# First two expert blocks turned by a one-hot product of x instead of a gather, in a two-layer block kernel on one Trainium2 core

## The reference, cut to what matters

```python
xn = rmsnorm(x, norm2_g)                    # [512, 1024]; x times 1/rms of its row times a gain
logits = xn @ w_router + b_router           # 4 groups, then 8 experts in the best group
top two experts of each token, with softmax weights
xs = xn[row_tok]                            # tokens sorted by expert, in blocks
ys = (silu(xs @ w_gate[e]) * (xs @ w_up[e])) @ w_down[e]     # 32 experts, hidden width 512
out = x + sum over a token's two experts of weight * ys
```

## Time and profile before

| | |
|---|---|
| runs, median of 3 | 1725.02 us (1723.73 to 1726.02) |
| the profiled execution, its own time | 1727.39 us |
| its span in the trace | 1725.5 us |
| PE busy | 1634.2 us, 95% |
| DVE busy | 742.6 us, 43% |
| ACT busy | 378.8 us, 22% |
| POOL busy | 191.5 us, 11% |
| HBM read and written | 298.60 MB and 15.73 MB |

### The profile page before, as it was taken

How to read it: one execution, slowest core, us unless ns; L and a number is a source line. 1 busy time by engine, 2 the same in 40 slices (tenths; PEclk the granted TensorE clock), 3 DMA queues, 4 the chain that set the end, 5 groups by cost and what they waited for, 6 DMA issues and landing times.

```text
span 1725.5 us, 17923 instructions
## 1 busy us (share of the span) xinstructions
PE 1634.2 (95%) x6932; PEld 943.7 (55%) x6932; DVE 742.6 (43%) x1517; ACT 378.8 (22%) x810; POOL 191.5 (11%) x206
## 2 busy tenths in 40 slices
PE   7999999999999999999999999997799998888986
PEld 4444454578888888855444788444333333333332
DVE  3386886465445454343774555256221211111111
ACT  4443754410000000022563223002111111010110
POOL 0000000000000000010002323150122211121211
PEclk9999999999999999999999999998799999998998
DMA  5531114030222212222121104539699999999993
GB/s 184 125 71 49 50 50 147 1 110 12 87 98 98 92 56 97 98 69 92 50 73 64 58 28 135 195 104 416 245 361 400 403 409 403 400 394 418 400 404 114
DMA packets 69089, 304.51 MB, mean 176 GB/s; under 512 B 10735, under 2 KB 11892, under 8 KB 55948
## 3 DMA queue, kind: packets, MB, share of 16 engines
q1 hardware_dynamic: 60416, 287.40, 43.1%
q0 software_dynamic: 7840, 13.80, 3.8%
q10 hardware_dynamic: 748, 2.15, 0.3%
HBM read 298.60 MB, written 15.73 MB: 182 GB/s over the span
## 4 chain that ended last, share of the span: by engine, by line
PE 85%; DMA 12%; DVE 2%; issue 1%; ACT 0%; POOL 0%; POOLq 0%; SPq 0%; DVEq 0%; ACTq 0%
PE ps L1589 11%; PE ps L1151 11%; PE ps L1195 11%; PE ps L1019 8%; PE ps L1292 7%; DMA W<-in_w_expert_up 6%; PE ps L1439 5%; PE ps L1604 5%; PE ps L1055 3%; PE ps L1015 3%; PE ps L1478 3%; PE ps L1504 2%; DMA yT<-in_w_expert_up 2%; DMA mix<-in_w_expert_up 2%; PE ps L1303 2%; PE ps L1074 1%
## 5 line engine op out<-in xcount | busy, mean ns | idle before, releaser
L2907 DVE SCALAR_TENSOR_TENSOR smb<-smb,ptb,ps 64x512 f32<-64x512 f32 x36 | 40.5, 1125 | 316.1 <-ACT smb L2044 316.0
L1589 PE MATMUL ps<-W,gb 128*64 128x512 f32 x480 | 138.5, 638 | 19.2 <-DMA W<-in_w_expert_up 14.2
L1589 PE MATMUL ps<-W,ptb 128*64 128x512 f32 x464 | 137.2, 632 | 15.3 <-DMA W<-in_w_expert_up 12.0
L1019 PE MATMUL ps<-W 128*128 128x512 f32 (+1 forms) x336 | 149.3, 596 | 1.5 <-ACT W L1721 1.5
L1292 PE MATMUL ps<-W 128*128 128x512 f32 x272 | 122.3, 599 | 1.9 <-DVE yT L2569 1.9
L1151 PE MATMUL ps<-yT,W 128*128 128x256 f32 x512 | 113.0, 379 | 0.0
L1604 PE MATMUL ps<-W,ptb 128*64 128x512 f32 x464 | 107.7, 606 | 1.4 <-ACT smb L2050 0.9
L1195 PE MATMUL ps<-W,mix 128*128 128x256 f32 x496 | 108.5, 379 | 0.0
L1151 PEld LDWEIGHTS ps<-yT,W 128*128 128x128 f32 x512 | 97.3, 190 | 13.2
L1019 PEld LDWEIGHTS ps<-W 128*128 128x128 f32 (+1 forms) x336 | 61.2, 188 | 75.0 <-issue 72.9
L1195 PEld LDWEIGHTS ps<-W,mix 128*128 128x128 f32 x496 | 94.2, 190 | 12.8
(11 more groups left out here) (456 smaller groups left out, 2415.4 us busy)
## 6 DMA issues: line engine op xcount, KB each, us to landing
W<-in_w_expert_up SPq DMA_DIRECT2D x25, 2048.0 KB, 29.5
W<-in_w_expert_down SPq DMA_DIRECT2D x25, 2048.0 KB, 34.0
W<-in_w_expert_gate SPq DMA_DIRECT2D x24, 2048.0 KB, 42.4
W<-in_w_in SPq DMA_DIRECT2D x16, 2048.0 KB, 7.7
W<-in_w_up SPq DMA_DIRECT2D x8, 2048.0 KB, 8.2
W<-in_w_down SPq DMA_DIRECT2D x8, 2048.0 KB, 7.9
W<-in_w_out SPq DMA_DIRECT2D x4, 2048.0 KB, 7.9
yT<-in_w_expert_gate SPq DMA_DIRECT2D x3, 2048.0 KB
```

The source lines that it names most:

```text
L1019: ins = pe.matmul(ps[0:n, bank, :], wv[:, k, j * P:j * P + n], hT[:, k, :], start=(k == 0), stop=(k == KT - 1))
L1589: ins = pe.matmul(ps[64 * part:64 * part + 64, 2, :], xsT[s][:, k, :], w[part][:, k, :], start=(k == 0), stop=(k == KT - 1))
L2907: dve.scalar_tensor_tensor(out=hid.rearrange("r (k p) -> r p k", k=4), in0=sgate.rearrange("r (p k) -> r p k", k=4), scalar=slot_weight[:, ...
```

## The change

1. **x product.** The turned tokens of blocks 0 and 1 no longer come from a gather. TensorE multiplies x, as it lies in SBUF, with `first_hot` of both experts side by side: 8 column groups of x times 4 token tiles, 32 products with 128 columns each, into banks 0 and 1 of PSUM. DVE multiplies block 0's half by the gain while it copies it (`first_rows`, two halves of four groups), ACT block 1's (eight small ACTIVATEs). The product takes x unscaled: each token's 1/rms and its expert weight come out of four more products (`r_first_w`, 3 columns), ACT copies them to `first_scale`, and they are applied as the scale of the silu and the scalar of `hidden`.
2. **Weight layout.** x is used with plain feature groups, so the gate and up pieces of experts 0 and 1 (m = 0, 1, 3, 4) are loaded by another pattern (`by_place`): eight runs of 2 KB for a partition instead of one of 16 KB.
3. **Normed rows of tiles 2 and 3** are made by ACT (times 1/rms) and POOL (times the gain), not by DVE; DVE only makes the reciprocals (`root`). ACT stores them to `h_scratch` after the first blocks' tokens.
4. **Order on SP.** `fixed(9)` goes first, `fixed(10)` waits for the x product (`first_cols`). The first half of piece 11 no longer waits for `job_ready`.
5. **Order on DVE and PE.** `job_ready` moves ahead of the slots; it needs two transposes that TensorE now does after the first half of the first `gate_up`. `row_ids` follow block 0's hidden rows. `xsT[1]` now lies in `cmask`, the tables in `fmask`.

```diff
@@ sync @@
+            by_place = [io[nm_].rearrange("l e (k p) n -> (l e) p k n", p=P) for nm_ in names]
             def fixed(m):
-                sp.dma_start(weights(m), source[m % 3][m // 3]).then_inc(piece_load[m], 16)
+                src = by_place if m // 3 < 2 and m % 3 < 2 else source
+                sp.dma_start(weights(m), src[m % 3][m // 3]).then_inc(piece_load[m], 16)
...
-            sp.wait_ge(turn_src, 4 * NORM[T_N2] + NT)
-            sp.wait_ge(turn_done, turned_by(T_N2, NT - 1))
-            sp.wait_ge(out_store, 16 * NT)
-            fixed(10)
             sp.wait_ge(logits_done, 5)
             fixed(9)
-            sp.wait_ge(job_ready, 1)
+            sp.wait_ge(row_scaled, 2)
+            sp.wait_ge(out_store, 16 * NT)
+            sp.wait_ge(first_cols, 2)
+            fixed(10)
...
+            sp.wait_ge(first_half, 1)
+            half_of(SPLIT[0], SPLIT[0] // 3, 0).then_inc(piece_load[SPLIT[0] % N_PIECES], 16)
+            sp.wait_ge(job_ready, 1)
             which = expert_at(FIXED)
-            for half in range(2):
-                sp.wait_ge(*((ex["gu"], 1) if half else (first_half, 1)))
-                for m in SPLIT:
-                    half_of(m, which if m // 3 == FIXED else m // 3, half).then_inc(piece_load[m % N_PIECES], 16)
+            half_of(SPLIT[1], which, 0).then_inc(piece_load[SPLIT[1] % N_PIECES], 16)
+            sp.wait_ge(ex["gu"], 1)
+            half_of(SPLIT[0], SPLIT[0] // 3, 1).then_inc(piece_load[SPLIT[0] % N_PIECES], 16)
+            half_of(SPLIT[1], which, 1).then_inc(piece_load[SPLIT[1] % N_PIECES], 16)
@@ gpsimd @@
+            for i in (2, 3):
+                pool.wait_ge(row_scaled, i - 1)
+                row = stage[:, i % 2, :].rearrange("p (k q) -> p k q", k=KT)
+                pool.tensor_tensor(row, row, gb[:, :].rearrange("p (q k) -> p k q", k=KT), ALU.mult).then_inc(turn_src, 1)
             pool.wait_ge(ids_ready, 1)
             for s in range(2):
                 pool.wait_ge(h_store[s], 16 * (NT // 2))
...
-            for s in range(2):
-                gather_tokens(s)
-            pool.wait_ge(ids_ready, 2)
             for n in range(2, 5):
-                fetch(n, n % 2, n - 1)
+                fetch(n, n % 2, n - 3)
@@ tensor @@
-            take(3)
+            take(0, 1)
             pe.wait_ge(first_ready, 1)
-            for e in range(2):
+            for k in range(KT):
                 for i in range(NT):
-                    ins = pe.matmul(ps[0:BLK, 3, 2 * e:2 * e + 2], first_hot[:, 2 * i + e, :], tokid[:, :, i],
-                                    start=(i == 0), stop=(i == NT - 1))
+                    ins = pe.matmul(ps[:, k // 4, (k % 4) * P:(k % 4 + 1) * P], x[:, i, k * P:(k + 1) * P],
+                                    first_hot[:, 2 * i:2 * i + 2, :], start=(i == 0), stop=(i == NT - 1))
+                if k % 4 == 3:
+                    ins.then_inc(first_cols, 1)
+            take(2, 3)
+            pe.wait_ge(first_ready, 2)
+            for i in range(NT):
+                ins = pe.matmul(ps[:, 3, 0:3], first_hot[:, 2 * i:2 * i + 2, :].rearrange("p e r -> p (e r)"), r_first_w[:, i, :],
+                                start=(i == 0), stop=(i == NT - 1))
             ins.then_inc(idT_done, 1)
...
-            pe.wait_ge(gather[0], 16)
-            turn_tokens(0)
...
                 if n == 0:
                     half_done.then_inc(first_half, 1)
+                    turn_tables()
...
                 if n == 0:
                     all_slots()
-                pe.wait_ge(gather[1 - s], 16 * ((n + 1) // 2 + 1))
-                turn_tokens(1 - s)
+                else:
+                    pe.wait_ge(gather[1 - s], 16 * ((n + 1) // 2))
+                    turn_tokens(1 - s)
@@ scalar @@
-            logits_copy(0)
-            keep_row(2)
-            for t in range(1, NT):
+            for t in range(NT):
                 logits_copy(t)
-            keep_row(3)
+            for i in (2, 3):
+                q = 4 * NORM[T_N2] + i
+                act.wait_ge(root_ready, i - 1)
+                act.wait_ge(h_store[i % 2], 16)
+                act.activation(stage[:, i % 2, :].rearrange("p (k q) -> p q k", k=KT), x[:, i, :].rearrange("p (q k) -> p q k", k=KT),
+                               ACT.Copy, scale=rstd[:, q:q + 1]).then_inc(row_scaled, 1)
...
+            act.wait_ge(ex["xT"], 1)
+            for k in range(KT):
+                ins = act.activation(xsT[1][:, k, :], ps[:, k // 4, (k % 4) * P + BLK:(k % 4 + 1) * P], ACT.Copy,
+                                     scale=gcol[:, 6, k:k + 1])
+            ins.then_inc(ex["xT"], 1)
+            then(act.activation(std[:, 0:1], epsc[:, 0:1], ACT.Silu))
+            keep_row(2)
+            keep_row(3)
@@ vector @@
-            norm_stage(T_N2, 2)
+            root(2)
...
-            norm_stage(T_N2, 3)
+            root(3)
...
+            dve.wait_ge(turn_src, 4 * NORM[T_N2] + NT)
+            first_rows(0)
...
-            dve.wait_ge(idT_done, 1)
-            token_ids(idcol[:, 0:2], ps[0:BLK, 3, 0:4].rearrange("p (e c) -> p e c", c=2)[:, :, 0], id_work[:, 0:2]).then_inc(ids_ready, 1)
+            first_rows(1).then_inc(ex["xT"], 1)
```

More of the change, by code:

```diff
@@ L261, in build @@
         idcol = sb("idcol", [BLK, 4], I32)
-        tables = cmask[0:1, 0:MAXJOBS + NE].bitcast(I32)
+        tables = fmask[0:1, 0:MAXJOBS + NE].bitcast(I32)
         jobs, placed = tables[:, 0:MAXJOBS], tables[:, MAXJOBS:]
@@ L292, in build @@
         r_blk, r_slot = work(2 * NT), work(2 * NT)
+        r_both, r_first_w = work(2, NT, 2), work(NT, 3)
         place_hot = gb[:, 0:2 * NT * BLK].rearrange("p (n r) -> p n r", n=2 * NT)
@@ L299, in build @@
         ys = flat_s[0:64, :].rearrange("p (s d) -> p s d", s=2)
[L300 removed]
+        xsT = [v.rearrange("p (k t) -> p k t", k=KT) for v in (gb[:, 512:1024], cmask[:, :])]
         hidT = ptb[:, 1, 0:256].rearrange("p (k t) -> p k t", k=4)
@@ L1657, in _ @@
                     gate_up(0, again, range(4, KT))
-                    pe.wait_ge(gather[0], j * 16 + (8 * STATIC + 32))
+                    pe.wait_ge(gather[0], j * 16 + (8 * STATIC + 16))
                     turn_tokens(0)
@@ L2031, in _, with hidden_silu @@
                     act.activation(r_x2, r_dv, ACT.Exp).then_inc(route_act, 1)
-            def first_tokens(n):
-                act.wait_ge(ex["xt"], n + 1)
-                for half in range(2):
-                    ins = act.activation(xsT[n][:, 4 * half:4 * half + 4, :],
-                                         ps[:, half, 0:4 * 96].rearrange("p (k t) -> p k t", k=4)[:, :, 0:BLK], ACT.Copy)
-                ins.then_inc(ex["xT"], 1)
-            first_tokens(0)
+            act.wait_ge(idT_done, 1)
+            act.activation(first_scale[0:64, 0:1], ps[0:64, 3, 2:3], ACT.Copy)
+            act.activation(first_scale[64:128, 0:1], ps[0:64, 3, 0:1], ACT.Copy)
+            act.activation(first_scale[0:64, 1:2], ps[64:128, 3, 2:3], ACT.Copy)
+            act.activation(first_scale[64:128, 1:2], ps[64:128, 3, 1:2], ACT.Copy).then_inc(first_w, 1)
+            act.wait_ge(ex["xT"], 1)
[6 more added lines that the diff above has]
+            keep_row(3)
+            act.wait_ge(first_w, 1)
             act.wait_ge(slots_ready, 2)
-            def hidden_silu(n):
+            def hidden_silu(n, scale=None):
                 act.wait_ge(ex["gu"], n)
-                act.activation(sgate, ps[0:64, 2, :], ACT.Silu).then_inc(ex["silu"], 1)
+                if scale is None:
+                    act.activation(sgate, ps[0:64, 2, :], ACT.Silu).then_inc(ex["silu"], 1)
+                else:
+                    act.activation(sgate, ps[0:64, 2, :], ACT.Silu, scale=scale).then_inc(ex["silu"], 1)
             def rows(n, s, shared=False):
@@ L2831, in _, with first_rows @@
                               ALU.is_equal).then_inc(first_ready, 1)
-            dve.wait_ge(rank_done, 2)
+            then(dve.tensor_tensor(r_both, msel[:, 0:2, :, 0:2], bc(wpos[:, :, :], 2), ALU.mult))
+            then(dve.tensor_tensor(r_first_w[:, :, 0:2], r_both[:, 0], r_both[:, 1], ALU.add))
+            roots = rstd[:, 4 * NORM[T_N2]:4 * NORM[T_N2] + NT]
+            dve.tensor_copy(r_first_w[:, :, 2], roots)
+            dve.tensor_tensor(r_first_w[:, :, 0:2], r_first_w[:, :, 0:2], bc(roots, 2), ALU.mult).then_inc(first_ready, 1)
+            dve.wait_ge(rank_done, 2)
+            def first_rows(half):
+                dve.wait_ge(first_cols, half + 1)
+                return dve.tensor_tensor(xsT[0][:, 4 * half:4 * half + 4, :],
+                                         ps[:, half, :].rearrange("p (k t) -> p k t", k=4)[:, :, 0:BLK],
+                                         bc(gcol[:, 6, 4 * half:4 * half + 4], BLK), ALU.mult)
             def token_ids(dst, src, work_):
@@ L2878, in _ @@
             then(dve.scalar_tensor_tensor(out=r_slot, in0=r_blk, scalar=float(-BLK), in1=rows8, op0=ALU.mult, op1=ALU.add))
```

(7 more changed lines are left out.)

66 lines of the change are left out of this document (34 added, 32 removed).

## The result

The changed kernel takes 1729.22 us (median of 8 runs, 1727.17 to 1733.5), the kernel before 1725.0 us beside it (median of 8, 1723.73 to 1726.02). The ratio is 1.0026, with a 95% interval of 1.0017 to 1.0035: 4.2 us slower, where 7.1 us faster was forecast. The profiled execution of the changed kernel took 1729.64 us, its span is 1727.8 us. Distances inside the stage are not touched by that.

A forecast was written before the change was run, and what follows sets the result against it. The weight stream was taken to set the end, through the load issued at 1257.65 after block 1's down product. The steps summed to 7.1 us off that event: 1725.0 - 7.1 = 1717.9 us, range 1713.5 to 1724.

The forecast's parts named there:

- What bounds the kernel: End of the kernel: set by the weight stream, through the load issued at 1257.65 when block 1's down product is done.
- step 7: Weight loads: queue holds 14.4 MB from 1212, done at 1248; the event at 1250.5 still rules, gains capped near 10 us.
- Steps 1, 2 and 3: Logits: routing 1.3 us sooner; x product done at 1210.7; first gate and up at 1211.7, 3.8 earlier, taking 7.0 us.
- The rival of the low clock: TensorE's clock stays low through the x product, 13.4 us; no gain, 1725 us; chance 10%.
- step 2: The x product on TensorE: 12 products in 5.1 us at low clock, then 20 in 4.2, done at 1210.7.
- Step 4: DVE stands twice at `first_rows`; slots, ready at 1220.2, come last ahead of block 0's silu; hidden rows done at 1222.0.
- Step 8: POOL's two rows, 2.35 us each from 1193.4, are done by 1199, before DVE asks after 1203: hidden.
- POOL and DVE hold each other up: Rival in the routing: DVE at worst stands for POOL's two products, 4.7 us; gain 2.4, 1722.6 us; chance 7%.
- Step 6: Block 2's gather: stores issued about 1216.3, landing at 1227, rows there at 1235.6, just in time; bounds no wait and 5.7 us.
- 1719 to 1724: Rival: block 2's gather is late by one to six microseconds, giving this time in us; chance 15%.
- Step 5: Block 0's down product takes 4.5 us; second gate and up starts at 1227.7 instead of 1234.8, 7.1 us earlier.

The follow-up runs named there:

- e4: The changed kernel, but POOL multiplies the rows of tiles 2 and 3 by 1.0 (one tensor input) instead of by the gain; 1724.38 us, ratio to before 0.9998.
- e9: e3, with DVE copying block 0's second half of the turned tokens after the table columns instead of ahead of them; 1718.89 us, ratio to before 0.9965.
- e1: The changed kernel, but POOL's two row products wait until DVE has made the first tokens' weights; 1723.67 us, ratio to before 0.9993.
- e2: The changed kernel, but DVE makes the rows of tiles 2 and 3 while waiting for the x product; 1723.0 us, ratio to before 0.999.
- e0: The changed kernel run again, unaltered; 1729.21 us, ratio to before 1.0026.
- e5: The kernel before, with four idle two-input POOL products started when the router's logits are done; 1724.59 us, ratio to before 0.9998.
- e3b: The changed kernel, with ACT's stores of tiles 2 and 3 issued right behind its second Exp; 1723.13 us, ratio to before 0.999.
- e3: e2 with e3b's edit, the early stores, added; 1719.85 us, ratio to before 0.9965.

## Why the prediction was wrong

**What bounds the kernel, and step 7: right.** From the load of piece 16 to the end were 466.8 to 468.5 us in all ten traces, while the load itself moved between 1248.62 and 1260.43. The change was worth at the end what it was worth at that event, in both directions.

**Steps 1, 2 and 3: right.** (Times of the first trace of the changed kernel.) The routing starts at 1194.67, 16.0 us after the out projection's last group, where before it was 17.35: 1.3 earlier, as taken. The x product took 9.79 us, and 8.73 to 10.12 in the other kernels, for 9.3, with the granted clock rising inside it. Gate and up then runs high, twice 3.65 us. Without the hold (in e4 with 1.6 us of it) it starts at 1211.43 to 1213.42 for the 1211.7 forecast. The rival of the low clock didn't come. That transposes do not engage the high level stands in the Trainium skill in Part 4 of TensorE: Matmul & The Clock Gate, not in Part 1 as step 2 has it, and no run here tests it.

**Step 4: right.** DVE waits 5.22 and 2.00 us at `first_rows`, and the silu of block 0 is released by the slots; e9 shows that they came last, since the silu starts earlier once they are ready sooner.

**Step 8 failed:** "POOL's two rows [...] are done by 1199, and DVE asks for them after 1203: hidden." It looked at who waits for the result, and the cost was in what the instructions do while they run. POOL's product took 2.83 us instead of 2.35, and DVE stood for both, 5.3 us; e1 shows it by moving them, e2 by giving the rows to DVE, and e4 removes 3.7 of the 5.3 us by another instruction on POOL. The rival had the mechanism ("POOL and DVE hold each other up") and nearly the size, 4.7 us, but 7% for a chance. What spoke against it was L2754, which has one input in PSUM: a row that couldn't show the case, as the prediction itself said. It should have had no weight. The Trainium skill (SBUF — State Buffer, SBUF: two separate sides) says that a DVE instruction with two SBUF inputs and a GpSimd instruction that reads SBUF lock each other out for the whole of the one that starts first; the pairs of e0 and e5 agree, and e1 has no such pair. e4 does not agree, since there DVE's two instructions took 0.90 and 1.01 us beside POOL's of 2.77 us, and others with two inputs passed in 0.19.

**Step 6 failed too, in its value, not in its bounds.** In e1, where the stores are issued at 1216.73 as forecast (1216.3), they land at 1230 and not at 1227, and the gather takes 8.28 us, not 7.4:

```profile
1216.73 0.33 ACTq L2020
...
1217.10 12.86 DMA h_scratch<-stage
...
1231.25 8.28 DMA stage<-h_scratch,idcol
```

That is the chain of e1 in order of time. The 12.86 us are nearer to the 14.28 of the earlier trace rows, which also ran beside weight loads, than to what was taken. The step says that "by either the sum has no wait"; but with the 14.28 of its own row the rows land at 1230.6 + 1.2 + 7.4 = 1239.2, 3.5 us after the 1235.7 at which they are due. The wait was 2.98 us. With the hold ahead of it it was 2.40 and 4.28. What the step didn't have is that a low clock level can follow such a wait: after those of 3.61 (e4) and 4.28 us (e0) the transposes took 1.54 us, after those of 2.16 to 2.98 us 0.88.

**The rivals were priced one at a time.** Each failure alone left a gain of some microseconds by its own reckoning (1722.6, and 1719 to 1724), and that is about what e3b and e1, with one of them each, measured (1723.13 and 1723.67). Both together came out above before, and no case held both. In e0, counted from the out projection's last group, piece 16 is issued 9.4 us later than the steps have it: 4.2 are there at the second gate and up, by the hold less some smaller gains, and 5.2 come after it, by the wait and the low stretch.

**The base of the sum was mixed.** The profiled execution of before was 2.4 us above the median, and the steps took their gain from its trace but subtracted it from the median. The trace has two low stretches that need not be there: down at 5.35 us where e5, otherwise the same kernel from there on, shows 3.65, and a longer third gate and up; e5's load of piece 16 is at 1254.16, 3.5 us earlier than the earlier trace rows. Whether the median execution has them isn't shown. Step 5 counts 0.85 us of the first as gained (5.35 to 4.5) and carries the second along as it is, so by the sum's own terms 0.85 us at most are gained where the median execution may have had nothing to lose; the rest of the 2.4 us is not explained.

**Step 5's 7.1 us came out of other terms.** Against its own execution the forecast was 1727.39 - 7.1 = 1720.3, and e3, which has neither loss, took 1720.15 in its profiled execution. That is in part luck. Its second gate and up starts at 1229.84, 2.1 us later than the 1227.7 of step 5: the first started 1.1 us later, the way from its start to the down product was 0.4 us longer, and the down product ran low, 0.7 us more than was taken. Its third gate and up then ran high, 1.7 us shorter than in before, which step 5 had carried along as it was; the load is at 1251.10 for 1250.5. Step 5's gain at the second gate and up was therefore 4.9 us in e3 (9.1 in e9, where the down product ran high). The best figure for the x product with its order, and the rows on DVE, is e3's: 4.8 us in the medians, 4.0 to 8.1 by the interval, which the 7.1 lies inside.

What stays open: what sets the level of the clock in block 0's down product and in the third gate and up, which differs between kernels that do the same there, and for the down product between two executions of one kernel; whether it is POOL's second input or its instruction that holds DVE to the end; and how much of the 9.4 us between the changed kernel and e3 belongs to each loss, since they overlap.

## What to carry to other kernels

Work moved to an idle engine is not hidden because nobody waits for its result: look at what the engine that sets the pace does in the same microseconds, and look for instructions that last longer than their like, since a hold like this one shows as busy time and not as a wait. A change that takes a wait away also takes the cover from everything that lay under it, so what was free before, here a routing with 3.15 us of slack, has to be priced anew. Rivals that can occur together have to be priced together. A store that somebody will wait for belongs where the queue is empty: the same 512 KB took 2.6 to 3.5 us there and 7.8 to 14.3 beside the weight loads. Where before's own trace holds an unlucky stretch, build the sum against a trace without it, or don't take its gain off the median.

## What the runs showed of the hardware that was not expected

- A DVE instruction of 0.17 us beside a two-input product of POOL took 2.87 us and ended with POOL's (1199.06 against 1199.0). In e5 the held ones were TENSOR_TENSOR with both inputs in SBUF, and one TENSOR_SCALAR (1.23 us); the TENSOR_REDUCE between them passed in 0.17, as did a TENSOR_TENSOR at 1197.66 that began as one POOL instruction followed another. One with an input in PSUM passed in 0.31 us (L2786 at 1194.97, as in before).
- POOL's product of 128x1024 took 2.83 us with the gain read through a view in steps of eight elements, 2.35 in the earlier trace rows, and in e4 2.77 with the row alone, which lies in order. So one input was not faster than two; how much of each is the view, the instruction or DVE beside it is not separated.
- Beside weight loads the second of two stores of 512 KB issued together took 11.08 us in the changed kernel and 12.86 in e1 (the first 7.8 and 9.5), against 14.28 for one in the earlier trace rows. With no load in the queue each took 2.6 us in e3, and 2.6 and 3.5 in e3b.
